# Two transformer blocks on one core: the order of work at the hand-overs between matrix products

## The reference

```
block 1:  h = rms_norm(x) @ w_in -> gated linear attention + sparse attention
          x = x + rms_norm(mixed @ w_out)
          h = rms_norm(x);  f = (silu(h @ w_gate) * (h @ w_up)) @ w_down
          x = x + rms_norm(f)
block 2:  z = rms_norm(x) @ w_in_2 -> a, gate, q, k, v
          conv = silu(layer_norm(depthwise_conv31(a * sigmoid(gate)) + bias))
          attn = neighbourhood attention on the 8 x 64 token grid (8 heads)
          x = x + [conv, attn] @ w_out_2
          h = rms_norm(x);  x = x + (silu(h @ w_gate_2) * (h @ w_up_2)) @ w_down_2
```

## Time and profile before

| | us |
|---|---|
| median of 3 runs | 1553.95 (1551.8 to 1554.38) |
| the profiled execution | 1554.4 |
| its span | 1552.4 |
| PE busy | 1506.3 (97%) |
| DVE, ACT, POOL busy | 659.7, 586.3, 653.6 |
| mean granted PE clock | 0.986 of full speed |

### The profile page before, as it was taken

One profiled execution on the slowest core, in us unless ns is written; L12 is line 12 of the kernel. 1 busy time (PEld: TensorE's weight loads), 2 busy tenths in 40 slices (PEclk: granted clock), 3 DMA queues, 4 the chain that ended last, 5 costly groups with the idle time before them and its releaser, 6 DMA issues.

```text
span 1552.4 us, 20374 instructions
## 1 busy us (share of the span) xinstructions
PE 1506.3 (97%) x7376; PEld 1192.7 (77%) x7376; DVE 659.7 (42%) x1095; ACT 586.3 (38%) x914; POOL 653.6 (42%) x302
## 2 busy tenths in 40 slices
PE   7999999999999988999999998999999999999998
PEld 6888788666668876888888885777667888888887
DVE  5212444775543456333331006777736433333001
ACT  4131332655462334222332224566654322232221
POOL 3433312663234433444445442665324444444443
PEclk9999999999999989999999998999999999999999
DMA  4522211111113322333333332421112333333333
GB/s 168 170 82 68 81 54 41 42 54 43 55 55 95 95 70 80 95 95 96 100 101 96 109 109 88 129 68 55 54 50 86 95 95 95 96 97 102 102 105 109
DMA packets 40893, 135.04 MB, mean 87 GB/s; under 512 B 4464, under 2 KB 8816, under 8 KB 40576
## 3 DMA queue, kind: packets, MB, share of 16 engines
q1 hardware_dynamic: 39504, 130.56, 28.1%
q10 hardware_dynamic: 1328, 3.64, 0.7%
HBM read 132.09 MB, written 2.10 MB: 86 GB/s over the span
## 4 chain that ended last, share of the span: by engine, by line
PE 70%; issue 19%; DVE 4%; POOL 4%; ACT 2%; DMA 0%; POOLq 0%; DVEq 0%; SPq 0%; ACTq 0%
PE bank L1033 18%; PE bank L1035 18%; PE bank L1034 18%; POOL wL L423 4%; PE bank L1062 2%; PE bank L1064 2%; PE bank L1063 2%; PE bank L1332 1%; PE bank L1333 1%; PE bank L1334 1%; DVE bank L1971 1%; PE bank L1202 1%; PE bank L1236 1%; PE bank L1197 1%; ACT wH L512 1%
## 5 line engine op out<-in xcount | busy, mean ns | idle before, releaser
L423 POOL TENSOR_TENSOR wL<-raw,wH 128x1024 fp32r<-128x1024 f32 x235 | 573.5, 2441 | 843.7 <-ACT wH L512 663.6
L512 ACT ACTIVATE wH<-raw 128x1024 fp32r<-128x1024 f32 x209 | 221.3, 1059 | 639.1 <-PE bank L1035 585.9
L1033 PE MATMUL bank<-aH,wH 128*128 128x512 f32 x1024 | 406.2, 397 | 13.6 <-POOL wL L423 7.5
L1035 PE MATMUL bank<-aH,wL 128*128 128x512 f32 x1024 | 400.8, 391 | 0.0
L1034 PE MATMUL bank<-aL,wH 128*128 128x512 f32 x1024 | 400.6, 391 | 0.0
L1033 PEld LDWEIGHTS bank<-aH,wH 128*128 128x128 f32 x1024 | 193.6, 189 | 64.4 <-issue 16.0
L1034 PEld LDWEIGHTS bank<-aL,wH 128*128 128x128 f32 x1024 | 193.7, 189 | 41.3 <-issue 2.0
L1035 PEld LDWEIGHTS bank<-aH,wL 128*128 128x128 f32 x1024 | 193.4, 189 | 40.6
L1033 PE MATMUL bank<-fH,wH 128*128 128x512 f32 x352 | 137.3, 390 | 0.0
L1034 PE MATMUL bank<-fL,wH 128*128 128x512 f32 x352 | 137.0, 389 | 0.0
L1035 PE MATMUL bank<-fH,wL 128*128 128x512 f32 x352 | 137.0, 389 | 0.0
(11 more groups left out here) (275 smaller groups left out, 1850.7 us busy)
## 6 DMA issues: line engine op xcount, KB each, us to landing
raw<-in_w SPq DMA_DIRECT2D x235, 512.0 KB, 3.5
bmk<-in_bias SPq DMA_DIRECT2D x6, 512.0 KB, 4.8
pj<-in_x SPq DMA_DIRECT2D x4, 512.0 KB, 6.5
out_x<-z2T SPq DMA_DIRECT2D x8, 256.0 KB, 3.5
ct<-in_ct ACTq DMA_DIRECT2D x3, 384.0 KB, 3.1
w1k<-in_w1k ACTq DMA_DIRECT2D x1, 1024.0 KB, 5.9
w1v<-in_w1v ACTq DMA_DIRECT2D x1, 1024.0 KB, 5.2
pv<-in_pv ACTq DMA_DIRECT2D x1, 128.5 KB, 4.6
```

Of the source, the lines that this page charges most:

```text
L423: pool.tensor_tensor(wL[:, c_slot, :], raw[:, c_slot, :], wH[:, c_slot, :].bitcast(F32), ALU.subtract).then_inc(sem("w_lo"), 1)
L512: act.activation(wH[:, s, :], raw[:, s, :], ACT.Copy).then_inc(sem("w_hi"), 1)
L1033: pe.matmul(bank[:], hi, H[:, ka, :], start=(k == 0), stop=False)
L1035: mm = pe.matmul(bank[:], lo, H[:, ka, :], start=False, stop=(k == p.k - 1))
```

## The change

1. `pg`: the first sigmoid of the gates stands behind the first chunk conversion, not ahead of the phase.
2. `rsqrt` writes the guess into a PSUM bank, and the Newton step reads it there (norms 2, 3, 4, 5 and 7; norms 1 and 6 pass no bank). The three products of a step are grouped so that each has the guess as an operand.
3. gu1: chunk conversions stand where their slot comes free: the first whole tile's after two squares, the next ahead of the root, the others among the SiLUs of the first two rounds. The sum over channels runs after four blocks of the first whole tile.
4. in2: all residuals first, then all low parts. PE takes both products of the first tile's high activation parts block by block, with the sums; then the same for the second tile, beside the first tile's products of the low parts; then the second tile's. The norm's root comes ahead of the first conversion on ACT.
5. The cleared borders of the conv's input are cleared alone.
6. The conv's SiLU is x/2 (1 + tanh(x/2)): DVE scales and shifts, ACT takes tanh, DVE multiplies. Its four channels are interleaved with the softmax steps 11 to 13. The root is spread some products earlier. tanh and exp share a table.
7. out2 and gu2: two conversions each stand one block earlier on ACT.

```diff
@@ ACT
-            gate(sg, KD)
-            gemm(PH["pg"], mid=gate_and_split)
+            gemm(PH["pg"], mid=(lambda: gate(sg, KD), gate_and_split))
-            def rsqrt(n, bank, width, summed, r=nr[:]):
+            def rsqrt(n, bank, width, summed, r=nr[:], guess=None):
-                act.activation(r, r, ACT.Exp, scale=-0.5).then_inc(sem("nr_ready"), 1)
+                act.activation(r if guess is None else guess, r, ACT.Exp, scale=-0.5).then_inc(sem("nr_ready"), 1)
                 square(2 * KD + kt, lambda: xT[:, kt, :])
+                if kt == 1:
+                    ahead(PH["gu1"], 2)
                 if by_k:
-                    ahead(p, 2)
+                    ahead(p, 3)
                     rsqrt(*norm)
-                    ahead(p, 3)
+                    act.preload_act_table_set("silu_and_others")
+                    ahead(p, 0, 1)
                     silu(0, 0)
                     high_f(0, 0)
                     silu(0, 1)
+                    ahead(p, 1, 1)
+                    high_f(0, 1)
+                    silu(1, 0)
+                    high_f(1, 0)
+                    ahead(p, 2, 1)
+                    silu(1, 1)
+                    ahead(p, 3, 1)
+                    high_f(1, 1)
...
+            rsqrt(5, B[6][:], D, (sem("sum_ready"), 5), nr[:], B[5][:])
             for t in range(1, NT2):
                 ahead(p, t - 1)
-                if t == 1:
-                    rsqrt(5, B[6][:], D, (sem("sum_ready"), 5))
...
+            act.preload_act_table_set("exp_and_others")
+            def tanh_of_conv(j):
+                act.wait_ge(sem("conv_x"), j + 1)
+                act.activation(sq[:, j % 2, :], yT[:, j, :], ACT.Tanh, scale=0.5).then_inc(sem("conv_tanh"), 1)
+            def high_of_conv(j):
+                act.wait_ge(sem("conv_silu"), j + 1)
+                act.activation(aH[:, j, :], yT[:, j, :], ACT.Copy, scale=0.5).then_inc(sem("conv_hi"), 1)
             probabilities(10)
             over_sums(10)
+            tanh_of_conv(0)
             probabilities(11)
-            act.preload_act_table_set("silu_and_others")
+            high_of_conv(0)
             over_sums(11)
-            for j in range(4):
-                if j == 2:
-                    ahead(q, 0)
-                act.wait_ge(sem("conv_val"), j + 1)
-                act.activation(yT[:, j, :], yT[:, j, :], ACT.Silu, scale=vec("ln_g", j), bias=vec("ln_b", j))\
-                    .then_inc(sem("conv_silu"), 1)
-                act.wait_ge(sem("conv_silu"), j + 1)
-                act.activation(aH[:, j, :], yT[:, j, :], ACT.Copy).then_inc(sem("conv_hi"), 1)
-            act.preload_act_table_set("natural_log_exp_and_others")
+            tanh_of_conv(1)
+            high_of_conv(1)
             values(3, 0)
+            ahead(q, 0)
+            tanh_of_conv(2)
             probabilities(12)
+            high_of_conv(2)
             over_sums(12)
+            tanh_of_conv(3)
             values(3, 1)
+            high_of_conv(3)
             ahead(q, 1)
...
-            for t in range(3):
+            for t in range(2):
                 square_and_high(t)
             ahead(q, 4)
-            square_and_high(3)
+            for t in range(2, 4):
+                square_and_high(t)
...
-            for t in range(4, KD):
+            for t in range(4, KD - 1):
                 square_and_high(t)
             ahead(q, 7)
+            square_and_high(KD - 1)
@@ PE
-            total(3 * KD, B[5])
             for t in range(4, 8):
-                tile_products(p, 0, t, 1, aH, aL, alone=B[gu1_bank(t)], idle=t < 6)
+                tile_products(p, 0, t, 1, aH, aL, alone=B[gu1_bank(t)], idle=t < 6,
+                              after=(lambda k: total(3 * KD, B[5]) if k == 3 else None) if t == 4 else None)
-            tile_products(p, 0, 0, 1, aH, aL, "h3_lo", after=add_up)
+            for k in range(KD):
+                pe.wait_ge(sem("h3_hi"), k + 1)
+                pe.matmul(bank0[:], wH[:, s0, b], aH[:, k, :], start=(k == 0), stop=False, skip_group_check=True)
+                pe.matmul(bank0[:], wL[:, s0, b], aH[:, k, :], start=False, stop=False, skip_group_check=True)
+                add_up(k)
...
+            for k in range(KD):
+                pe.matmul(bank1[:], wH[:, s1, b], aH[:, k, :], start=(k == 0), stop=False, skip_group_check=True)
+                pe.matmul(bank1[:], wL[:, s1, b], aH[:, k, :], start=False, stop=False, skip_group_check=True)
+                pe.wait_ge(sem("h3_lo"), k + 1)
+                mm = pe.matmul(bank0[:], wH[:, s0, b], aL[:, k, :], start=False, stop=(k == KD - 1), skip_group_check=True)
+            mm.then_inc(sem("chunk_done"), 1)
+            for k in range(KD):
+                mm = pe.matmul(bank1[:], wH[:, s1, k * P:(k + 1) * P], aL[:, k, :], start=False, stop=(k == KD - 1), skip_group_check=True)
+            mm.then_inc(sem("chunk_done"), 1)
...
-                if slot == 21 and b == 1:
+                if slot == 20 and b == 3:
                     spread_root(3, B[7])
@@ DVE
-                link(dve.scalar_tensor_tensor(t, r, -0.5, r, ALU.mult, ALU.mult))
-                link(dve.tensor_tensor(t, t, x, ALU.mult))
-                link(dve.scalar_tensor_tensor(r, t, 1.5, r, ALU.add, ALU.mult))
+                link(dve.tensor_tensor(t, guess[:], x, ALU.mult))
+                link(dve.scalar_tensor_tensor(t, t, -0.5, guess[:], ALU.mult, ALU.mult))
+                link(dve.scalar_tensor_tensor(r, t, 1.5, guess[:], ALU.add, ALU.mult))
...
-                    if kt:
+                    if kt and not lows_last:
                         low_of_x(use, next_gain, kt - 1)
-                low_of_x(use, next_gain, KD - 1)
+                for kt in range(0 if lows_last else KD - 1, KD):
+                    low_of_x(use, next_gain, kt)
...
             normed(3, 0)
+            dve.wait_ge(sem("root_spread"), 3)
+            dve.wait_ge(sem("ln_cen"), 4)
+            def scaled(j):
+                dve.scalar_tensor_tensor(yT[:, j, :], yT[:, j, :], vec("ln_g", j), B[7][:], ALU.mult, ALU.mult)\
+                    .then_inc(sem("conv_val"), 1)
+                dve.wait_ge(sem("conv_val"), j + 1)
+                dve.tensor_scalar(yT[:, j, :], yT[:, j, :], vec("ln_b", j), None, ALU.add).then_inc(sem("conv_x"), 1)
+            def silu_of_conv(j):
+                dve.wait_ge(sem("conv_tanh"), j + 1)
+                dve.scalar_tensor_tensor(yT[:, j, :], sq[:, j % 2, :], 1.0, yT[:, j, :], ALU.add, ALU.mult)\
+                    .then_inc(sem("conv_silu"), 1)
+            def low_of_conv(j):
+                dve.wait_ge(sem("conv_hi"), j + 1)
+                dve.scalar_tensor_tensor(aL[:, j, :], yT[:, j, :], 0.5, aH[:, j, :].bitcast(F32), ALU.mult, ALU.subtract)\
+                    .then_inc(sem("conv_lo"), 1)
+            scaled(0)
             masked_max(11)
-            dve.wait_ge(sem("root_spread"), 3)
-            for j in range(4):
-                dve.wait_ge(sem("ln_cen"), 4)
-                dve.tensor_tensor(yT[:, j, :], yT[:, j, :], B[7][:], ALU.mult).then_inc(sem("conv_val"), 1)
-                if j == 1:
-                    over_sums(11)
+            silu_of_conv(0)
             copied(10)
+            over_sums(11)
+            scaled(1)
+            low_of_conv(0)
             normed(3, 1)
+            silu_of_conv(1)
+            copied(11)
+            low_of_conv(1)
+            scaled(2)
+            masked_max(12)
+            silu_of_conv(2)
+            over_sums(12)
+            scaled(3)
+            low_of_conv(2)
+            silu_of_conv(3)
+            masked_max(13)
+            low_of_conv(3)
             clear_sum(7)
-            low_of("conv", lambda j: yT[:, j, :], range(4))
-            copied(11)
-            masked_max(12)
-            over_sums(12)
-            masked_max(13)
             copied(12)
```

More of the change, by code:

```diff
@@ L531, in body @@
                             q += 1
[L532 to L533 removed]
+                        if mid is not None and t < 2:
+                            mid[t]()
                         if evict is not None:
```

60 lines of the change are left out of this document (34 added, 26 removed).

## The result

The changed kernel took 1533.12 us (median of 4 runs, 1531.98 to 1533.84) against 1552.88 for the kernel before in the same comparison (4 runs, 1551.8 to 1554.38). The ratio is 0.9872, with a 95% interval of 0.986 to 0.9884. The forecast was 1539.2, from 1535.0 to 1544.5: the direction was right and the gain was larger than the range allowed. One execution each of e10 (1879 us), of e14 (3593) and of the kernel before (3010) is left out of all medians and clocks.

A forecast was written before the change was run, and what follows sets the result against it. PE was taken as the bound, fed without a gap between phase hand-overs, so savings there move the end. Terms 0.5 + 7.0 + 1.2 + 3.5 + 2.6 = 14.8 took 1554.4 to 1539.6, forecast as 1539.2, range 1535 to 1544.5.

The forecast's parts named there:

- pg, 0.5: In pg, the sigmoid behind the first chunk conversion ends the third tile's wait for POOL: 0.5 us gained.
- Guesses in PSUM, 1.47 each: At the ends of out1 and dn1, the narrow Newton op no longer waits for POOL: 1.47 us saved at each.
- 3.5 - 1.1: Before gu1's tile 6, PE's old wait of 3.5 us shrinks to 1.1 through the new conversion order.
- gu1, 7.0: From out1's end through gu1, an earlier root, shorter waits and less half clock gain 7.0 us in sum.
- the 0.5 at tile 8: In gu1, chunks 7 to 9 converted between SiLUs may leave a 0.5 us wait at tile 8.
- half clock of 1.65: In gu1's tile 6, half clock behind the old wait cost 1.65 us and goes with that wait.
- in2's opening, 1.2: At in2's start, an earlier first product, mostly offset by a new 2 us wait before the third tile: 1.2 us gained.
- conv, 3.5: Around the conv, the new SiLU and its order remove most of PE's three waits for DVE: 3.5 us gained.
- out2, gu2, 2.6: At out2's end and in gu2, earlier conversions remove PE's waits for POOL: 2.6 us gained.
- the term for the attention stage: In the attention stage, half clock was taken to stay at mean 0.96, a 5.6 us loss, so no gain.
- rival 2: The attention stage loses half of its low clock, 2.8 of the 5.6 us, giving 1536.4; chance 0.12.
- rival 3: Half clock returns at new places, behind waits in in2 or gu1: up to 4.1 us less gain, 1543.3; chance 0.15.

The follow-up runs named there:

- e10: The kernel before with the fourth pair's head sums three blocks later in in2's last tile; 1554.6 us, ratio 1.0014.
- e14: The changed kernel with in2's first chunk slot freed earlier in the second pass and the third pair's head sums two blocks later; 1530.4 us, ratio 0.9854.
- e5: The changed kernel with the five guesses written back into SBUF, all orders kept; 1540.2 us, ratio 0.9914.
- e16: The kernel before with only the guesses in PSUM and the Newton step regrouped; 1545.2 us, ratio 0.9946.
- e4: The kernel before with 12 more products in dn1's sixth tile, which put everything behind later; 1553.1 us, ratio 0.9994.
- e13: The kernel before with the third pair's head sums two blocks later in in2's sixteenth tile; 1550.4 us, ratio 0.9977.
- e2: The kernel before with in2's opening alone changed, guesses in SBUF; 1552.0 us, ratio 0.9991.
- e1: The changed kernel with in2's old opening alone put back, guesses still in PSUM; 1537.1 us, ratio 0.9895.
- e9: The changed kernel run again with nothing changed; 1535.0 us, ratio 0.9878.
- e18: The changed kernel run once more with nothing changed; 1535.4 us, ratio 0.9883.
- e3: The changed kernel with 12 more products in dn1's sixth tile, which put everything behind later; 1536.9 us, ratio 0.9897.
- e6: The changed kernel with the conv's old SiLU, its order among the softmax steps and its root's spread put back; 1536.8 us, ratio 0.9895.
- e11: The changed kernel with in2's first chunk slot freed earlier and the fourth pair's head sums three blocks later; 1537.0 us, ratio 0.9881.
- e8: The changed kernel with in2's second pass reordered so that the first chunk's slot is free earlier; 1536.2 us, ratio 0.9883.

## Why the prediction missed

- **pg, 0.5.** Right: 0.5.
- **Guesses in PSUM, 1.47 each.** Right at both narrow roots (0.16 for 1.63, and e5 brings 1.63 back). That the wide norms gain nothing for PE except where told was wrong as a reading of the kernel before: by e16 the wide root of gu1 alone carried 2 us of tile 6's wait. So the guesses are worth more than the 2.9 that they had, and gu1's order less. The sum is right nevertheless, since the 3.5 - 1.1 was counted once, under the order.
- **gu1, 7.0.** 8.0 measured. Tile 6's wait was forecast at 1.1 and is 0.8 (0.95 more between starts than a product takes); the 0.5 at tile 8 did not come, PE has no wait there. The half clock behind out1, assumed to stay, is nearly the same behind the restart (4.9 us for 5.4), but the spread ahead of it left half clock: 0.7 in all. The half clock of 1.65 was put down to the 3.5 us wait. It is gone, but it is less tied to the wait than I wrote: e4 and e13 have that wait and no such fall, while e2 and e10 have both.
- **in2's opening, 1.2.** The mechanism came as written. The first product is 948.22 - 936.83 = 11.4 earlier, less the 8.5 that the stages ahead had gained 2.9, for a forecast of 2.8. The new wait before the third tile, forecast at 2, is 1.8. The reordering alone is worth little: by the distances, without the fall behind the new wait, from 0.9 less (e1 against e9 and e18; 0.7 less for e2 against the kernel before) to 0.7 more (e1 against the first profile), and 0.3 more from e16 to the changed kernel, whose half clock behind the restart is equally long (3.1 and 3.0 us). The root gives the rest. 2.3 was measured, 0.9 of it because half clock was over 3.0 us behind the restart, and not 5. In e9 and e18 it lasted 6.2 and 6.1, so that 0.9 was luck, and 5 is about the mean of the three.
- **conv, 3.5 and out2, gu2, 2.6.** 3.3 and 2.9. The waits left for the conv's low parts are 0.5 and 0.2, for a forecast of 0.7.
- **What failed** is the term for the attention stage, priced at no change with a mean clock of 0.96, a loss of 5.6 us. The stage's falls cost 5.1 in the kernel before, nothing in the first profile and 1.7 in e9's and e18's. I had read one profile and taken its falls for a property of the kernel. The other case stood as rival 2, with half of the loss for 0.12. Over the twelve executions, the mean loss to the clock is (1 - 0.9916) x 1532 = 12.9 us, against (1 - 0.9872) x 1552 = 19.9 before. Of these 7.0 us I had 1.65. The surplus of 5.3 answers to the surplus of the medians, 1554.0 - 1534.3 - 14.8 = 4.9, though clock lost while PE stands idle costs nothing and so the two need not agree this closely.
- **The reading under it** was incomplete. I wrote that the trace shows half clock behind a wait once, behind the 3.5 us of gu1, and used that against rival 3. But the larger fall of the attention stage (1076 to 1083) begins in the sixteen products right behind a wait of 1.56:

```profile
1075.16 2.85 PE L1343 MATMUL bank<-ct,sq 128*128 128x2 f32 x16 [1.56 <-ACT VS L881]
```

Why the changed kernel loses less is shown in part only. Fewer and shorter waits of PE leave fewer places for a fall (e13, e14, e16, and the table of all profiles): it lost tile 6's wait and the conv's, and took on the one of 1.83. The root stall ahead of in2's restart seems to count: with the guess in SBUF, windows of 2 us around the restart, idle ones included, lose 5.1 in all six profiles (the kernel before, e2, e4, e5, e10, e13); with it in PSUM they lose 3.4 in eight of fourteen and 5.1 in the others. At out1's end it is 5.1 in three of the six, and 3.4 in all fourteen. And chance counts, from one execution to the next (e3, e9, e18). How much of the 7.0 each has, these runs don't settle.

The Trainium skill (TensorE: Matmul & The Clock Gate, "HAM oscillation — how this bites in real kernels") tells of a kernel in which a recurring wait for DMA, of some 3 to 5 us, brings the low clock back every time. Here a wait of 3.25 us did so in three of five profiles and one of 1.57 us in nine of sixteen, and one program differed in it from execution to execution (e3, e9).

## What to carry to other kernels

Price a tuned kernel's clock as a spread and not as one profile's figure: look at several executions before the half clock of a stage goes into a sum as fixed. A DVE op on a chain that PE waits for should have an operand in PSUM where POOL works beside it; this one edit gave 8.2 us of the 20, about half of it through the clock. Where an opening is reordered, ask what frees the next weight slot: three blocks ahead, then the products that close the first tile, took the new wait away, and the gain showed in the time only when the next wait, 100 us on, went too.

## What the runs showed of the hardware

- The same program (e3, four executions), with the same waits, ran at 1534.3 or 1539.4 us, nothing between, at a mean clock of 0.993 or 0.990. Where PE has work, a fall to 1.2 GHz costs 1.6 to 1.7 us, or two or three times that; where PE waits for others it costs less (e13 at 1118: 1.0 for 3.4).
- Half clock follows waits of PE much shorter than gu1's 3.25: 1.83 us (five of ten profiles), 1.57 (nine of sixteen), 0.4 (six of twenty). The same sixteen narrow products without a wait had none behind them (0 of 40).
- A narrow (128x4) DVE op with both inputs in SBUF took 1.63 us beside POOL's subtraction and 0.16 with one input in PSUM (e5, the changed kernel); a wide one (128x512) 2.77 and 0.69 (the kernel before, e16).
- 12 more products (2.7 us of work) made the kernel before no slower: 1553.1 against 1554.2 (0.9984 to 1.0004), the clock at 0.9889 against 0.9870.
- Ahead of all that was changed, the profiles lose 3.4 us of clock at 112 to 122 and none at 322 (twelve of twenty), 1.7 at each of the two places (e1, e5, e6, e11, e13, e16) or 3.4 and 1.7 (e4, e8). Even an unchanged part has no fixed clock.
